# Ends of the feed-forwards and the sine layers of the Hyena filter: VectorE's last steps in another order, two modulation turns and the sine layers later

## What is computed

```python
# block 1, layers 0 and 1 (mixers: SSM with attention, Conformer convolution)
mod = silu(c) @ mod_w[layer] + mod_b[layer]         # sh1, sc1, g1, sh2, sc2, g2
h = rms_norm(x, norm_g[layer, 1]) * (1 + sc2) + sh2
g = causal_dwconv(h @ w_gate, dw_w, dw_b)           # 1024 -> 2816, 3 taps
x = x + g2 * ((silu(g) * (h @ w_up)) @ w_down)
# block 2, layers 0 and 1 (mixers: latent attention, Hyena)
z = dwconv3(h @ w_up_2, conv_w, conv_b); a, g = split(z, 2)
x = x + g2 * ((silu(g) * a) @ w_down)
# filter of the Hyena mixer
h = sin(f_freq1 * (z @ f_w1 + f_b1))                # first sine layer, 256 x 64
h = sin(f_freq2 * (h @ f_w2 + f_b2))                # second sine layer
h = h @ f_w3                                        # taps, then a decay window
```

## Time and profile before

| | |
|---|---|
| median of 3 runs | 1615.52 us (1615.09 to 1624.87) |
| span of the profiled execution | 1615.2 us |
| TensorE busy | 1510.7 us (94%) |
| VectorE busy | 1200.6 us (74%) |
| ScalarE busy | 732.9 us (45%) |
| granted TensorE clock, mean | 0.971 |

### The profile page before, as it was taken

The page is one execution under the profiler, slowest core; times in us unless marked ns, Lnnn a source line. Parts: engine busy times, 40 slices in busy tenths (PEclk is TensorE's granted clock), DMA queues, the critical chain, the costliest instruction groups (busy, mean ns, idle before and its releaser), DMA issues.

```text
span 1615.2 us, 29296 instructions
## 1 busy us (share of the span) xinstructions
PE 1510.7 (94%) x11372; PEld 1352.9 (84%) x11372; DVE 1200.6 (74%) x1901; ACT 732.9 (45%) x981; POOL 52.1 (3%) x38
## 2 busy tenths in 40 slices
PE   5698989999999889999989889999999999999998
PEld 2584488999988668999989766899999877899997
DVE  7999747888889945999985556386666869576665
ACT  2322345344454334544444666365545542355453
POOL 2501200000000000000000000000000000000000
PEclk9598999999999899999999999999999999999999
DMA  9334836887844663988832400335554533245551
GB/s 357 130 105 152 294 129 279 308 311 304 338 174 185 226 244 141 363 350 312 330 146 88 130 11 1 132 125 188 182 183 168 185 112 108 79 157 182 184 180 52
DMA packets 55190, 307.89 MB, mean 191 GB/s; under 512 B 6631, under 2 KB 7688, under 8 KB 30984
## 3 DMA queue, kind: packets, MB, share of 16 engines
q1 hardware_dynamic: 53272, 302.40, 50.7%
q10 hardware_dynamic: 1840, 4.41, 0.9%
HBM read 304.17 MB, written 1.05 MB: 189 GB/s over the span
## 4 chain that ended last, share of the span: by engine, by line
PE 76%; DVE 12%; ACT 5%; issue 3%; DMA 3%; DVEq 0%; POOL 0%; ACTq 0%; SPq 0%
PE bank L1904 60%; DMA raw<-in_stream 2%; PE bank L2302 2%; PE bank L1833 2%; PE bank L2139 2%; ACT w_hi L659 2%; DVE hf L1304 2%; PE bank L2268 2%; DVE h_lo L1313 1%; DVE w_lo L1131 1%; DVE rstd L1287 1%; PE bank L2286 1%; PE bank L2175 1%; PE bank L2154 1%; ACT arena L937 1%
## 5 line engine op out<-in xcount | busy, mean ns | idle before, releaser
L1904 PE MATMUL bank<-h_hi,w_hi 128*128 128x256 f32 x2184 | 630.8, 289 | 23.4 <-DVE h_lo L1313 18.1
L1904 PE MATMUL bank<-h_lo,w_hi 128*128 128x256 f32 x2184 | 622.7, 285 | 0.0
L1904 PE MATMUL bank<-h_hi,w_lo 128*128 128x256 f32 x2184 | 622.4, 285 | 0.0
L1131 DVE TENSOR_TENSOR w_lo<-raw,w_hi 128x2048 fp32r<-128x2048 f32 x186 | 426.4, 2294 | 126.2 <-ACT w_hi L659 125.1
L1904 PEld LDWEIGHTS bank<-h_hi,w_hi 128*128 128x128 f32 x2184 | 422.4, 193 | 36.1 <-DVE h_lo L1313 22.9
L659 ACT ACTIVATE w_hi<-raw 128x2048 fp32r<-128x2048 f32 x186 | 355.2, 1911 | 156.7 <-PE bank L1904 100.2
L1904 PEld LDWEIGHTS bank<-h_lo,w_hi 128*128 128x128 f32 x2184 | 422.8, 194 | 1.1 <-issue 0.7
L1904 PEld LDWEIGHTS bank<-h_hi,w_lo 128*128 128x128 f32 x2184 | 422.7, 194 | 0.0
L1904 PE MATMUL bank<-a_hi,w_hi 128*128 128x256 f32 (+1 forms) x760 | 221.8, 292 | 5.4 <-DVE a_lo L1502 5.4
L1904 PE MATMUL bank<-a_lo,w_hi 128*128 128x256 f32 (+1 forms) x760 | 219.6, 289 | 0.0
L1904 PE MATMUL bank<-a_hi,w_lo 128*128 128x256 f32 (+1 forms) x760 | 219.4, 289 | 0.0
(11 more groups left out here) (285 smaller groups left out, 1566.6 us busy)
## 6 DMA issues: line engine op xcount, KB each, us to landing
raw<-in_stream SPq DMA_DIRECT2D x186, 1024.0 KB, 4.9
arena<-in_mod_stream SPq DMA_DIRECT2D x64, 768.0 KB, 6.7
arena<-in_mod_later SPq DMA_DIRECT2D x48, 512.0 KB, 6.7
raw<-in_mod_pe SPq DMA_DIRECT2D x36, 512.0 KB, 6.5
arena<-in_mod_pe SPq DMA_DIRECT2D x12, 512.0 KB, 12.9
sq<-in_bias SPq DMA_DIRECT2D x8, 256.0 KB, 7.1
x<-in_x_t ACTq DMA_DIRECT2D x1, 1024.0 KB, 9.2
arena<-in_ctx_t SPq DMA_DIRECT2D x1, 1024.0 KB, 4.9
```

Of the source, the lines that this page charges most:

```text
L1131: nc.vector.tensor_tensor(w_lo[s][:], raw[s][:], w_hi[s][:].bitcast(F32), ALU.subtract).then_inc(lo_done, 1)
L1904: ins = nc.tensor.matmul(out_, l, r, start=first and n == 0, stop=last and n == 2, **kw)
```

## The change

```diff
@@ ScalarE, ffn(f)
                 if f == 2:
-                    filter_hidden(1)
-                if last:
-                    turns = 4
-                else:
-                    turns = 5
-                with act.Fori(0, turns) as i:
+                    filter_hidden(0)
+                with act.Fori(0, 4) as i:
                     run(2 * i + 1, q0 + 2, q0 + 5, i)
                     run(2 * i + 2, q0 + 5, q0 + 8, i)
-                if last:
-                    run(9, q0 + 26, q0 + 29)
-                    run(10, q0 + 29, q0 + 32)
+                run(9, q0 + 26, q0 + 29)
+                run(10, q0 + 29, q0 + 32)
@@ ScalarE
             projection_norm("mla_out", 11)
-            filter_hidden(0)
             ffn(2)
             norm_x(12, 12)
+            filter_hidden(1)
@@ VectorE, ffn(f)
                 if f == 2:
-                    filter_angle(1)
-                turns = 4 if last else 5
+                    filter_angle(0)
+                turns = 4
@@ VectorE, ffn(f), behind the loop
-                if last:
-                    run(9, q0 + 26, q0 + 29, None, {})
-                    run(10, q0 + 29, q0 + 32, None, {})
+                run(9, q0 + 26, q0 + 29, None, {0: 12, 2: 13})
+                g = step(10, q0 + 29)
+                next(g)
+                lo(q0 + 32)
+                next(g)
+                next(g)
+                for q in range(q0 + 33, min(q0 + 35, NQ)):
+                    lo(q)
+                    if b0 is not None:
+                        mod_block(b0 + 14 + q - q0 - 33, c0)
                 nxt[0] = q0 + 35
-                if b0 is not None:
-                    mod_block(b0 + 15, c0)
@@ VectorE
-            filter_angle(0)
             ffn(2, 3, None, None)
             norm(12)
+            filter_angle(1)
@@ TensorE, ffn(f)
                 first_up_gate(q0, h_of(FFN_NORM[f]))
-                if f == 2:
-                    filter_layer(1)
-                with pe.Fori(0, 5) as i:
+                with pe.Fori(0, 4) as i:
@@
+                for e in range(2):
+                    s, q = 9 + e, q0 + 26 + 3 * e
+                    up_gate(s, q)
+                    if b0 is not None and e:
+                        mod_turn_now(b0 + 13, 39)
+                    down(s - 1, q + 2)
+                    if b0 is not None and not e:
+                        mod_turn_now(b0 + 12, 36)
                 down(10, q0 + 32, last=True)
                 if b0 is not None:
-                    mod_turn_now(b0 + 15, 45)
+                    for b in (14, 15):
+                        mod_turn_now(b0 + b, 3 * b)
@@ TensorE
             norm_sum(12)
-            stay_awake(17)
+            filter_layer(1)
+            stay_awake(15)
```

## The result

| | kernel before | changed kernel |
|---|---|---|
| median of 20 runs each | 1619.86 us (1612.18 to 1624.87) | 1626.55 us (1621.58 to 1630.13) |
| ratio | | 1.0048, 95% interval 1.0037 to 1.0060 |
| profiled span | 1615.2 us | 1624.5 us |
| mean granted clock | 0.971 | 0.964 |

The change costs 0.48%, by the interval +6.0 to +9.7 us, and 6.7 us from median to median. The kernel before came out 4.3 us above the median of the three runs that the prediction started from. The pair of profiles differs by 9.3 us.

What follows compares the result with a forecast made beforehand. TensorE was taken to hold 76% of the chain, so only the seams between feed-forward and norm count. 4.6 + 1.2 + 4.4 - 4.0 - 0.3 + 1.2 = +7.1 on 1615.5 gave 1622.6 us, range 1616.5 to 1627.0.

Steps and rivals of the forecast that it cites:

- change 6: Sine layer ahead of the Hyena projection: delays ScalarE's first evacuation, so TensorE waits before the second tap matmuls, +1.2 us.
- Change 1: End of `ffn(0)`: VectorE waits idle for `a_hi`, where block 14 filled the time before; additions later, +4.6 us.
- Change 2: End of `ffn(1)`: same new order, VectorE waits for `a_hi` though the DMA is not late, +1.2 us.
- Change 3: TensorE idles behind the ends of `ffn(0)` and `ffn(1)`, so both norm sums restart at a low clock, +4.4 us.
- Rival A: The clock stays up in both tails, behind `ffn(0)` and `ffn(1)`: -4.4, 1618.2 us; chance 0.18.
- C: Straight code of 8 written-out steps not delivered in time on TensorE: 2.11 us each, 16.9 us, 1639.5 us; chance 0.05.
- D: Tails cost nothing and the Hyena delay is taken up: -4.3, 1611.2 us; chance 0.06.
- Change 4: Beginning of `ffn(2)`: second sine layer no longer precedes the first gate tap; TensorE's gap and low clock go, -4.0 us.
- Change 5: End of `ffn(2)`: `down(10)` starts earlier, of which only the wait of the last additions is saved, -0.3 us.
- rival B: The Hyena gap of 1.2 us cools the clock too: adds 1.7, 1624.3 us; about one in three, chance 0.17.
- Change 7: Two of ten feed-forward steps written out as straight code on TensorE instead of a loop turn: 0.

Runs made afterwards that it cites:

- 6: Changed kernel with ScalarE's `a_hi` of the last step ahead of the next chunk's split `hi`; 1626.17 us, 1.0054 to the kernel before.
- kernel 7: As 6, plus on VectorE block 14 ahead of the split behind `a_lo` and block 15 ahead of the last split; 1622.81 us, 1.0038 to before.
- kernel 4: Changed kernel with matmuls of zeros in TensorE's waits at the ends of `ffn(0)` and `ffn(1)`; 1619.58 us, 1.0011 to the kernel before.
- experiment 3: Kernel before with only steps 9 and 10 of every feed-forward written out, instruction order kept; 1618.46 us, 1.0001 to the kernel before.
- experiment 2: Changed kernel with the sine layers put back, so only the new ends and written-out steps; 1625.20 us, 1.0043 to the kernel before.
- kernel 1: Kernel before with only the sine layers moved as in the change; 1615.61 us, 0.9984 to the kernel before.
- 8: Kernel before with steps 9 and 10 written out in old order and both sine layers inside `ffn(2)`; 1614.67 us, 0.9980 to before.
- 10: As 8, with 16 matmuls of zeros in the wait ahead of the last 32 Hyena output matmuls; 1612.68 us, 0.9956 to the kernel before.

## Why the prediction was right and where it was not

Three steps of the sum failed: the base of 1615.5 us, the price and the chance of the low clock behind the gap of change 6, and the sentence that the effect "counts as no change".

**The base.** The effect was forecast at +7.1 us and measured at +7.8 (6.0 to 9.7), or +6.7 from median to median. The time, 1622.6 us, was 4 us short of 1626.55. The first step that failed is the last of the sum, "1615.5 + 7.1": the 1615.5 were the median of three runs that lay 0.4 and 9.4 us apart, two of them on the low side, and 20 runs have it at 1619.86. The one run at 1624.87 was in view and went into the range as drift, not into the centre. The range (to 1627.0) just holds the result. Within 1% was right.

**"Counts as no change": the second step that failed.** I took it that a measurement can tell only about 1% (16 us) from no change. With 20 runs of each kernel the interval is 1.0037 to 1.0060, some 0.12% to either side, so the 0.48% is a measured slowdown and not a tie. The 7.1 us of my own sum lie in the interval, and I should have forecast a slower kernel.

**Change 1 (+4.6): right in kind, somewhat large.** The wait was 4.32 us and the delay of the additions 4.05 to 4.1. Five other profiles with this order wait 4.41, 4.39, 5.70, 4.36 and 3.50 us: the landing of the DMA moves it. That it is this landing and not ScalarE's order alone is shown by 6, and by 7 that block 14, put into the wait, saves it.

**Change 2 (+1.2): right.** 0.96 us of waiting, 1.05 of delay.

**Change 3 (+4.4): right, shown by 4.** From the start of the sum to `rstd` it is 1.99 and 2.38 us more in the first profile. Over the four profiles with this order and without zeros (sums of 5.70, 5.84, 5.49, 5.17 and of 6.40, 6.09, 5.48, 5.51 us) it is 1.8 and 1.9 on average, so 3.7. The bound "2.6 us at most" did not hold: the sums of 6.40 us, and of 6.59 and 6.76 in kernel 7, are 2.7 to 3.0 above 3.72. Rival A, the clock staying up in the tails, was seen in none of the four. Rivals C and D fell with experiment 3 and with the ends' cost in experiment 2.

**Change 4 (-4.0): right.** -4.05 in kernel 1. The gap and the low clock behind it went together, and what I called hidden was hidden.

**Change 5 (-0.3): too small.** -0.75 in kernel 2.

**Change 6 (+1.2): the third step that failed.** The gap is as forecast, 1.29 us, with the mechanism named: slack 0.15, sine ahead of the evacuation. But the low clock behind it belongs in the sum: I gave rival B one in three and 1.7 us; the clock fell in four of six profiles and that costs 3.2. Six profiles are few for the share; the price is the same in all four. The error was to take the price from the gap at 448, where 4 us were at the low clock; here it is some 7. On average the term is 1.3 + 4/6 x 3.2 = 3.4 us.

**Change 7 (0): right, shown by 3.**

In the prediction's own range the upper end, 1624.5, is 1 us too high: its bounds give 5.2 for change 3 and 1.3 for change 6, 1623.5 us.

With these sizes the sum is 4.1 + 1.05 + 3.7 - 4.05 - 0.75 + 3.4 = +7.5 us, against +7.8 by the ratio. The forecast of +7.1 was near because two errors met: change 6 was 2.2 too small, and the others together 1.8 too large. That part was luck.

**Left open.** The zeros took off more than their terms (6.0 and 3.9 us against 3.7 and, at four in six, 2.1), each within its interval. Whether they keep some later place at the full clock as well, these runs can't tell from chance; between 832 and 907 they did not (kernel 4). Kernel 7 shows 3.6 us less in its trace and 1.7 by the ratios, which stays open too.

## What to carry to other kernels

When work is moved out of a wait, ask what then fills the wait; block 14 cost nothing where it stood, and 4.1 us ahead of the additions once it stood behind. Price every new idle time of TensorE twice, once as the gap and once for the clock behind it: here 5 to 6 us of waiting for VectorE, free in themselves, cost about 2 us in each norm sum, and a gap of 1.3 us cost 4.4 to 4.5 in four profiles of six and 1.3 in two. TensorE can be given matmuls of zeros into a free bank for such a wait: in kernel 4 they brought both norm sums back to 3.72 us. A forecast that is to hold to a few us needs more than three runs for its base.

## What the runs showed of the hardware

A gap of 1.3 us ahead of the tap matmuls was followed by the full clock in two profiles and by some 7 us near the lower level in four, with the same instructions there. At the products behind a wait of 3.74 us, 32 matmuls took 7.1 us or 8.6 to 8.8 in kernels with the same code. At 280 the changed kernel itself, in its two profiles, had the full clock behind a wait of 1.22 us (11.61 us) and the lower one behind 1.28 us (13.09 us).

Three one-column matmuls at 452.49 and three at 459.12 did not keep the clock up (456 to 464 at 0.50), while 26 of zeros, 128x512, between them did (1.00).

Kernels 8 and 10 have the same code up to the last Hyena products, and at the end of `ffn(0)` they paid in different places. In 8, and in the kernel before, the gap ahead of `down(10)` was followed by the low clock (448 to 452 at 0.62 and 0.57), and the norm sum took 3.72 us. In 10 a gap of 1.36 us left it at 1.00, and then the norm sum was cold, at 5.41 us, behind waits of 0.92 and 0.68 us with three one-column matmuls between them (the stretch, then TensorE's timeline):

```profile
448.00:452.00 4.00, 4.00 (x36) 4.00 (x35) 4.00 (x7) 0.00 (x0) 0.00 (x0) 1.00 0.90 330
```

```profile
454.01 0.83 PE L1854 MATMUL bank<-ones,arena 128*128 128x1 f32 x6 [0.92 <-DVE arena L1172]
455.52 5.41 PE L1829 MATMUL bank<-sq,ones 128*128 128x256 f32 x16 [0.68 <-ACT sq L672]
```
